# Eight more pairs of gate tiles as Strassen units ahead of the attention stages, fewer as fill inside them

## What is computed

```
# first block, per layer
h = rmsnorm(x);  u = h @ w_in[i]                       # w_in: 1024 x 5120
sb_q, sb_k, sb_v, da_q, da_k, da_v, gate_a, gate_b = split(u)   # gates: 1024 wide each
y_a = stick_breaking_attention(sb_q, sb_k, sb_v) @ w_br_a       # 8 heads of 64
y_b = rmsnorm(differential_attention(da_q, da_k, da_v)) @ w_br_b  # 4 heads, two maps each
x = x + (sigmoid(gate_a) * y_a + sigmoid(gate_b) * y_b) @ w_o
x = x + moe(rmsnorm(x));  x = x + (p @ w_ple) * sigmoid(rmsnorm(x) @ w_ple_gate)
# second block
h = h + 0.5 * rms_norm(swiglu(rms_norm(h)))
proj = rms_norm(h) @ w_in     # latent q, kv, key; dilated q, k, v; gates: 2048 wide
o_a = dense_attention(...);  o_b = dilated_mixture(dq, dk, dv)     # 8 heads each
h = h + rms_norm((gates[0] * (o_a @ w_branch_a) + gates[1] * (o_b @ w_branch_b)) @ w_out)
h = h + 0.5 * rms_norm(swiglu(rms_norm(h)))
```

## Time and profile before

| | us |
|---|---|
| time, median of 3 runs | 3021.24 |
| lowest, highest | 3016.02, 3024.18 |
| span of the profiled execution | 3017.0 |
| TensorE busy | 2943.6 |
| VectorE busy | 1308.3 |
| ScalarE busy | 652.7 |
| GpSimd busy | 820.3 |
| stick-breaking, layer 2 (from, to) | 1021, 1111 |
| differential attention, layer 2 | 1111, 1212 |
| token-major units and dilated attention | 2199, 2385 |

### The profile page before, as it was taken

The page is one execution under the profiler, slowest core; times in us unless marked ns, Lnnn a source line. Parts: engine busy times, 40 slices in busy tenths (PEclk is TensorE's granted clock), DMA queues, the critical chain, the costliest instruction groups (busy, mean ns, idle before and its releaser), DMA issues.

```text
span 3017.0 us, 31787 instructions
## 1 busy us (share of the span) xinstructions
PE 2943.6 (98%) x12506; PEld 1884.5 (62%) x12506; DVE 1308.3 (43%) x2213; ACT 652.7 (22%) x1083; POOL 820.3 (27%) x625
## 2 busy tenths in 40 slices
PE   9999999999899999999998999999999999999998
PEld 7865464333468754643333688888664445888887
DVE  6733443111546435431225644433563464644442
ACT  2035313111210253231112300002112441300011
POOL 5400022222135000222222145542300102254442
PEclk9999999999999999999999999999999999999999
DMA  5211125999522101249996122222211201222220
GB/s 190 84 70 43 54 79 225 388 387 384 205 84 84 70 29 56 85 171 387 379 377 274 70 84 92 90 93 89 86 75 56 84 29 56 80 88 84 84 98 28
DMA packets 81379, 412.67 MB, mean 137 GB/s; under 512 B 25872, under 2 KB 26256, under 8 KB 34768
## 3 DMA queue, kind: packets, MB, share of 16 engines
q1 hardware_dynamic: 56608, 387.57, 33.7%
q0 software_dynamic: 24624, 23.08, 2.3%
HBM read 513.31 MB, written 31.46 MB: 181 GB/s over the span
## 4 chain that ended last, share of the span: by engine, by line
PE 67%; DVE 5%; ACT 1%; issue 1%; DMA 0%; DVEq 0%; POOL 0%; ACTq 0%
PE PS L1103 33%; PE PS L608 6%; PE PS L1037 5%; PE PS L1276 3%; PE PS L569 3%; PE PS L594 3%; PE PS L1059 3%; PE PS L686 2%; PE PS L840 1%; PE PS L895 1%; PE PS L516 1%; PE PS L1339 1%; PE PS L1011 1%; PE PS L1319 1%; PE PS L781 1%
## 5 line engine op out<-in xcount | busy, mean ns | idle before, releaser
L3086 POOL TENSOR_TENSOR ATT<-ring 128x512 f32<-128x512 f32 (+1 forms) x98 | 128.0, 1306 | 1203.4 <-PE PS L1103 689.8
L1103 PE MATMUL PS<-G,ATT 128*128 128x256 f32 x1360 | 321.6, 379 | 0.0
L1103 PE MATMUL PS<-HT,ring 128*128 128x256 f32 x1392 | 317.8, 379 | 3.8 <-ACT HT L2626 2.1
L1103 PE MATMUL PS<-G,ring 128*128 128x256 f32 x1232 | 291.4, 379 | 0.0
L1103 PEld LDWEIGHTS PS<-HT,ring 128*128 128x128 f32 x1392 | 264.1, 190 | 43.6 <-issue 3.5
L1103 PEld LDWEIGHTS PS<-G,ATT 128*128 128x128 f32 x1360 | 258.4, 190 | 36.4 <-issue 0.9
L608 PE MATMUL PS<-HT,ring 128*128 128x512 f32 x576 | 263.2, 600 | 0.0
L2808 ACT ACTIVATE TMP<-PS 128x256 f32<-128x256 f32 x92 | 35.2, 383 | 1053.2 <-PE PS L1103 935.9
L1103 PEld LDWEIGHTS PS<-G,ring 128*128 128x128 f32 x1232 | 234.1, 190 | 31.8
L1037 PE MATMUL PS<-ring,G 128*64 128x512 f32 x1024 | 226.8, 595 | 0.6 <-ACT G L2777 0.6
L608 PEld LDWEIGHTS PS<-HT,ring 128*128 128x128 f32 x576 | 104.5, 190 | 126.6 <-issue 120.2
(11 more groups left out here) (383 smaller groups left out, 4370.0 us busy)
## 6 DMA issues: line engine op xcount, KB each, us to landing
ring<-in_stream SPq DMA_DIRECT2D x163, 1024.0 KB
ring<-in_experts_gu SPq DMA_DIRECT2D x128, 1024.0 KB
ring<-in_experts_down SPq DMA_DIRECT2D x64, 1024.0 KB
G<-expert_rows SPq DMA_DIRECT2D x8, 1024.0 KB, 7.6
h_tokens<-G POOLq DMA_DIRECT2D x2, 2048.0 KB, 7.6
XT<-in_xT SPq DMA_DIRECT2D x1, 1024.0 KB, 8.4
G<-in_pT POOLq DMA_DIRECT2D x2, 512.0 KB, 6.2
out_T<-XT SPq DMA_DIRECT2D x2, 512.0 KB, 3.7
```

Source lines behind the costliest of these rows:

```text
L1103: mm = pe.matmul(product(g, name), x[:, k * P:(k + 1) * P], y[:, k, :], start=first and k == 0 and name in opening, stop=last and k == h - ...
L3086: pool.tensor_tensor(a["S1"], a["A21"], a["A22"], ALU.add)\
```

## The change

`FIRST_GATES` goes from 4 to 8, so in each layer two more Strassen units stand ahead of stick-breaking attention. There 5 plain tiles are left in place of 6: two at the start and one in each of the cycles 0, 2 and 3 (`SB_PAIRS`). In differential attention 3 tiles are left in place of 6: half a tile in each of the steps 2, 3, 6, 7, 10 and 11 (`DA_FILL`). In the mixer four new Strassen units (`MIX_GATES`) follow the token-major units, and the dilated attention's steps get 8 tiles in place of 16 (`DIL_FILL`: step, then tile, first and last of its 8 matmuls): a half in the lead and in step 1, a quarter in steps 2 to 25, an eighth in steps 26 to 29, a quarter in 30 and 31. The other engines' lists follow. The mask table's load now waits for the last of the four new units, which belongs to the second set.

```diff
@@ -39,9 +39,14 @@
-FIRST_GATES = 4
-SB_TILES = 6
-DA_HALVES = 12
+FIRST_GATES = 8
+SB_PAIRS = (0, 2, 3)
+SB_TILES = 2 + len(SB_PAIRS)
+DA_FILL = (2, 3, 6, 7, 10, 11)
+MIX_GATES = 4
+DIL_FILL = {0: (0, 0, 4), 1: (0, 4, 8)}
+DIL_FILL.update({2 + n: (1 + n // 4, 2 * (n % 4), 2 * (n % 4) + 2) for n in range(24)})
+DIL_FILL.update({26 + n: (7, a, b) for n, (a, b) in enumerate(((0, 1), (1, 2), (2, 3), (3, 4), (4, 6), (6, 8)))})
 DA_BRANCH = (12, 13, 14, 14, 15)
@@ -125,12 +130,14 @@
     u += [quartered(w_in, 0, D, 672 + 256 * n) for n in range(4)]
-    u += [unit_of(w_in, 0, D, c, c + 256) for c in range(672 + 1024, w_in.shape[1], 256)]
+    u += [unit_of(w_in, 0, D, 672 + 1024 + 256 * n, 672 + 1280 + 256 * n) for n in range(2)]
+    u += [quartered(w_in, 0, D, 672 + 1536 + 256 * n) for n in range(MIX_GATES)]
+    u += [unit_of(w_in, 0, D, c, c + 256) for c in range(672 + 1536 + 256 * MIX_GATES, w_in.shape[1], 256)]
     return (u + cut(turned, MLA_H * ROPE_M) + cut(plain, MLA_H * NOPE) + cut(w_uk, 512) + cut(w_uv, 512)
...
-QUARTERED = (1, 2, 3, 6, 7, 8, 9, 12, 13)
+QUARTERED = (1, 2, 3, 6, 7, 8, 9) + tuple(range(12, 12 + FIRST_GATES // 2))
 N_LAYER_U = 20 + 2 + 2 + 4 + 1
@@ -806,12 +813,13 @@
                     log_weights(2 * j + 1)
+                    if j in SB_PAIRS:
+                        tile = 2 + SB_PAIRS.index(j)
+                        project_part(gates, HT, tile, 0, 2)
                     if 2 * j + 2 < SB_H:
-                        project_part(gates, HT, j + 2, 0, 2)
                         logits(j + 1)
-                        project_part(gates, HT, j + 2, 2, KD)
-                    else:
-                        project_part(gates, HT, j + 2, 0, KD)
+                    if j in SB_PAIRS:
+                        project_part(gates, HT, tile, 2, KD)
                     values(j)
@@ -913,8 +921,8 @@
                 def fill(u):
-                    if u < DA_HALVES:
-                        project_half(gates, HT, 2 * SB_TILES + u)
+                    if u in DA_FILL:
+                        project_half(gates, HT, 2 * SB_TILES + DA_FILL.index(u))
                     for m in branches_at(u):
@@ -1310,8 +1318,11 @@
                 quartered_unit(t0)
-            at["mix_generic"] = now.count("unit_done")
             quartered_tokens(t0)
+            for n in range(MIX_GATES):
+                quartered_unit(t0)
+                if at["items"][-1]["set"]:
+                    at["mix_generic"] = now.count("unit_done")
             pe.wait_ge(Q["tile_done"], 2 * (len(at["groups"]) - 1))
@@ -1319,7 +1330,8 @@
             def gate_fill(u):
-                project_half(gates, HT, u)
+                if u in DIL_FILL:
+                    project_part(gates, HT, *DIL_FILL[u])
             at["dil"] = now.count("lin_ready")
@@ -1678,8 +1690,8 @@
                     softplus(2 * j)
-                    if j:
-                        take_gate(FIRST_GATES + 1 + j, scaled=True)
+                    if j - 1 in SB_PAIRS:
+                        take_gate(FIRST_GATES + 2 + SB_PAIRS.index(j - 1), scaled=True)
                     suffix(2 * j)
@@ -2239,8 +2251,8 @@
                 def take_fill(u):
-                    if u < DA_HALVES and u % 2:
-                        take_gate(FIRST_GATES + SB_TILES + u // 2, scaled=True)
+                    if u in DA_FILL[1::2]:
+                        take_gate(FIRST_GATES + SB_TILES + DA_FILL.index(u) // 2, scaled=True)
                     for m in branches_at(u):
@@ -2367,10 +2379,14 @@
                     rope(KR, SWAP_16, ROPEM[:, 0, :], ROPEM[:, 1, :], TURN[:, 0:S])
+            for n in range(MIX_GATES):
+                dst = GF[:, 2 * n * S:(2 * n + 2) * S]
+                quarter_sums(g + 6 + n, dst)
+                by_rstd(dst, "dve_step")
             def take_gate_fill(u):
-                if u % 2:
-                    take_gate(u // 2, scaled=True)
+                if u in DIL_FILL and DIL_FILL[u][2] == KD:
+                    take_gate(2 * MIX_GATES + DIL_FILL[u][0], scaled=True)
             v.wait_ge(Q["toep_landed"], now.next("toep_landed", 16))
@@ -2659,7 +2675,8 @@
                 for j in range(SB_H // 2):
-                    order += [("gate", j + 2), ("values", j)]
+                    order += [("gate", 2 + SB_PAIRS.index(j))] if j in SB_PAIRS else []
+                    order += [("values", j)]
@@ -2865,7 +2882,7 @@
                 da0 = at[f"da{L}"]
-                order = fill_order(DA_H, 2, lambda u: (u < DA_HALVES and u % 2) + len(branches_at(u)))
+                order = fill_order(DA_H, 2, lambda u: (u in DA_FILL[1::2]) + len(branches_at(u)))
                 attention(DA_H, lambda qb: (qb + 1) * P, 2, 1.0, True,
@@ -2960,9 +2977,9 @@
             inverse_root(KVR, 7, RKV)
-            for i in range(6):
+            for i in range(6 + MIX_GATES):
                 first_product(at["mix"][1] + i)
-            dil = fill_order(MLA_H, 1, lambda u: u % 2)
+            dil = fill_order(MLA_H, 1, lambda u: u in DIL_FILL and DIL_FILL[u][2] == KD)
             mla = fill_order(MLA_H, 1, lambda u: u in MLA_BRANCH)
@@ -3144,7 +3161,7 @@
             pool.wait_ge(Q["t_ready"], at["mix"][2] + 4)
-            weight_sums(at["mix"][0], at["mix"][0] + 5)
+            weight_sums(at["mix"][0], at["mix"][0] + 5 + MIX_GATES)
             pool.wait_ge(Q["unit_done"], at["mix_generic"])
...
             pool.wait_ge(Q["pos2_landed"], 32)
```

## The result

The changed kernel takes 3085.57 us (median of 4 runs, 3083.79 to 3085.75) against 3019.38 us for the kernel before on the same chip: a ratio of 1.0216 with an interval of 1.0204 to 1.0228. The profiled execution's span is 3083.3 us, 66.3 longer than before. The mean granted clock fell from 0.996 to 0.986.

A forecast was written before the change was run, and what follows sets the result against it. TensorE was 98% busy, but the attention steps were held bound by other engines' chains. Layers +40.1, clock +15 and mixer +2.4 us made +57.5: 3074.5 us of span, 3078.7 us of time, range 3061 to 3093.

The forecast's parts named there:

- forecast A: Whole kernel: pauses are as long as the chains and the clock falls in most of them, 3078.7 us; 70%.
- Units: Layers: two added Strassen units cost 2 x 12.08 = 24.2 us per layer, with no wait added.
- Bare steps of differential attention: Six steps per layer lose their fill: pauses of 3.0 or 2.5 us, only 3.7 us saved for 20.6 of work.
- Stick-breaking: Cycle j = 1 without its tile: a pause of about 4.7 us, 0.4 us saved per layer.
- Clock: Layers: TensorE's clock falls behind new pauses, 2.0 us per differential head and 1.5 per stick-breaking pause, +15 us in all.
- rival B: The clock stays up in the differential heads, 3066.7 us, or everywhere, 3062.8 us; 16%.
- Mixer: Dilated attention with what surrounds it: +2.4 us, including 0.9 for half a chance of one clock fall.
- GpSimd beside VectorE: Mixer: GpSimd's sums for the first two gate units slow VectorE's rope, +0.8 us, bounds 0 and 3.
- Dilated steps: Mixer: steps with eight tiles removed give back 48.6 us, nearly the 48.3 added; odd steps last 2.51 us.
- The mask table's +1.1 us: Dilated stage's start: the table loads only after the last unit, delaying the first maxima by 1.1 us, bounds 0 and 2.5.
- C: Rival: the low clock lengthens chains and returns late, so a differential head costs 5 us instead of 2, 3097 us; 8%.
- D: Rival: the pauses don't open because VectorE finishes sooner, leaving only the saving of 13.3 us, 3008 us; 3%.

The follow-up runs named there:

- e_busy: The changed kernel with matmuls whose result nobody reads put into TensorE's pauses in differential, stick-breaking and dilated attention: 3065.73 us, ratio 1.0159 to the kernel before.
- e_less_work: The kernel before with 21 of 24 matmuls left out of three gate tiles in each differential stage, nothing added: 3039.13 us, ratio 1.0067.
- e_pool_later: `e_mixer` with GpSimd's sums for the new gate units held until VectorE's fourth rope is done: 3021.64 us, ratio 1.0005 to the kernel before.
- e_keys_later: `e_pool_later` with dilated step 0 filled, uneven dilated fills, and GpSimd's first four key multiplies held until VectorE took that stage's last values: 3012.17 us, ratio 0.9976.
- e_layers: The change in the two layers only, the mixer as in the kernel before: 3077.77 us against 3018.96, ratio 1.0196.
- e_mixer: The change in the mixer only, the layers as in the kernel before: 3027.05 us, ratio 1.0027.
- e_spread: The changed kernel with the same three gate tiles per differential attention spread over all twelve steps: 3069.72 us, ratio 1.0166 to the kernel before.

## Why the prediction was right, and where it was off

3078.7 us was forecast with a range of 3061 to 3093; 3085.57 came. The direction and the mechanism of forecast A hold. By its steps:

**Units.** 2 x 12.08 us per layer were forecast, 23.6 and 22.4 measured. Right to 1.8 us; the second number also holds what lies between the layers' attention.

**Bare steps of differential attention.** Waits of 3.0 and 2.5 us were worked out from the VectorE rows; 3.0 and 2.6 stand in the trace. The gain of 3.7 us per layer is 3.4 at full clock (`e_busy`). What it rests on, that the chain and not TensorE's work sets a bare step's length, is shown twice: `e_less_work` has the stage at 61.1 us with 18 us less work, and `e_busy` at 57.8 with useless work in it.

**Stick-breaking.** Pause 4.7 forecast, 4.68 measured; gain 0.4 forecast, 0.3 measured at full clock.

**Clock.** 15 us were charged to the layers, 19.3 measured (`e_busy` against the changed kernel). The term that was mis-sized is the 2.0 us per head: 16.2 us for six heads is 2.7 each. It was also put together wrongly. The sum had 1.7 us for a spell of full work and 0.3 for slower scores; in the first head the fill lost only 0.8 (4.47 for 3.70) and the scores inside the chain 1.7 (1.65 for 0.92 and 2.08 for 1.13), and in the second the head values lost 2.0 (4.33 for 2.32), which the sum had not counted. The row taken as pattern was a spell in which only scores and a turn stood. The bound of 3.4 us a head held. The Trainium skill's warning against long pauses ("TensorE: Matmul & The Clock Gate", "Why this matters for your kernels"), read to the letter, would have charged only the stick-breaking pause and was rival B: the trace is against that reading, since the clock fell in or right behind pauses of 2.58 us in the second and third head, and in the kernel before behind two of 1.2 and 1.1.

**Mixer.** +2.4 forecast, +11.4 measured up to the first latent scores. Three terms:
- GpSimd beside VectorE: +0.8 forecast, bounds 0 and 3, though the forecast's own two numbers, 3 us of delay against 2.8 us of slack, give 0.2; 6.2 measured, of which 3.5 are the wait and 2.7 the clock behind it. The prediction looked at the rope, and by its own rule should have looked at each VectorE operation with two SBUF inputs in the time GpSimd was newly busy. The rope was already beside GpSimd's sums in the kernel before (3.329 us); the five scale-and-add operations were what the new sums reached. `e_pool_later` shows it: holding the sums takes back all of the 6.
- Dilated steps: 48.6 us were to come back, 44.6 did. About 1.7 is the clock in step 1, 1.6 the last steps, where GpSimd's key multiplies now run beside VectorE's normalising (1.23 and 1.31 us for 0.49) with no four matmuls above it (`e_keys_later`), and the rest 0.05 us in each odd step (2.56 for 2.51).
- The mask table's +1.1 us came as forecast, and the clock fell behind the pause that it lengthens, for which the forecast had charged half a chance. It fell there in `e_layers` too, where the pause is as before.

The total is nearer than its parts: the layers' stages cost some 5 us more than forecast and the mixer 9.0, while the units cost 2.3 less and 3 us came back in stretches that the change doesn't touch. That is luck: no term of the forecast stands for it.

**Rivals.** B and C stand on either side of what came: the clock fell in all six heads and cost more than the forecast had, but 2.7 us a head and not C's 5. D would have needed bare steps with waits under 0.5 us; the least was 2.58. What stays open is how much of `e_less_work`'s 20 us is owed to the other routing; only its differential stage is used here. Open is also what decides whether the clock falls behind a pause of 0.8 to 2 us, since the same pauses have it in some traces and not in others.

The whole change can't be won in the layers at any clock: two units cost 24.2 us where the chains give back 3.4 + 0.3. In the mixer it can: from the first dilated to the first latent scores `e_keys_later` takes 130.5 us where the kernel before took 183.5, 53.0 us back for 48.3 added.

## What to carry to other kernels

Work that fills an engine's waiting time is free up to the end of the chain beside it. Before moving such work out, read from the trace when the other engine's last instruction ends: that is all that comes back, and whatever replaces the work is paid in full. A pause that opens on TensorE can be paid twice, once as idle time and once by the clock of what follows; if it can't be closed, spread the fill, or put matmuls there that nobody reads. And when an engine gets new work, list every instruction of its neighbour that now runs beside it, not only the one that was slow before.

## What the runs showed of the hardware

- The granted clock can fall from 2.4 to 1.2 GHz behind pauses as short as 1.2 and 1.1 us with a 0.66 us turn between them (the kernel before at 2424), but short pauses don't always bring it down: with 0.84 and 1.11 us at this place it fell in `e_layers` (2485 to 2488) and stayed at 1.00 in `e_mixer` (2431 to 2438). In differential attention it stays at 1.00 where 0.7 to 1.1 us of waiting remain in each bare step (`e_busy`). In `e_spread` it fell in a row of pauses of 1.1 to 2.45 us. Such a fall took 1.6 to 1.7 us in latent attention and about 2.7 in a head of differential attention.
- Useless matmuls pay: 35 of them in `e_busy` (2 in each of twelve bare steps, 4 in each of two stick-breaking cycles, 3 in the dilated stage), 0.86 us each, made the kernel 20 us faster (17 by the ratios).
- VectorE's scale in place (`tensor_scalar`, one SBUF input, 128x512) takes 1.23 to 1.31 us beside GpSimd's multiplies of 64x512 and 0.49 alone; its two-input multiply-and-add of 128x512 takes 1.87 us on average beside GpSimd's new sums and 1.17 with these held; a multiply of 128x1024 3.3 us beside GpSimd's sums of 128x1024 and 1.23 alone.
